# Sample attention rewritten: keys turned by VectorE, block-diagonal queries, 1 MB page gathers, prompt's merge inside the stage

## The reference, cut to what matters

```python
def dilated_window_sample(q, kv_buf, k_new, v_new, window, dilation):
    ...
    sc = jnp.einsum('bqhe,bqjhe->bhqj', q, g[:, :, :, 0]).astype(jnp.float32) * (e ** -0.5)
    p, den, lse = masked_softmax_parts(sc, valid[None, None])
    o = jnp.einsum('bhqj,bqjhe->bqhe', p, g[:, :, :, 1]) / jnp.swapaxes(den, 1, 2)[..., None]

def fox_sample(q, k_new, v_new, logf_new, k_past, v_past, logf_past):
    ...
    s_past = jnp.einsum('bqhe,bkhe->bhqk', q, k_past).astype(jnp.float32) * (e ** -0.5)
    s_past = s_past + cq - jnp.transpose(c_past, (0, 2, 1))[:, :, None, :]
    ...
    pr = jax.nn.softmax(jnp.concatenate([s_past, s_new], axis=-1), axis=-1)

def merge_branches(oa, ob, ga, gb, w_pa, w_pb, w_o):
    ya = oa.reshape(b, s, A_OUT) @ w_pa
    yb = ob.reshape(b, s, B_OUT) @ w_pb
    return (ga * ya + gb * yb) @ w_o
```

## Time and profile before

| | |
|---|---|
| median of 3 runs | 1204.61 us (1200.33 to 1204.88) |
| span of the profiled execution | 1184.3 us; the page has no time of its own beside it |
| median less span | 20.3 us |
| TensorE, VectorE, ScalarE, POOL busy | 1046.9, 333.7, 261.0, 243.6 us |
| `phase_c` | 387.5 to 750 us |
| merge in `phase_d` | 750 to 795 us |

### The profile page before, as it was taken

One profiled execution on the slowest core, in us unless ns is written; L12 is line 12 of the kernel. 1 busy time (PEld: TensorE's weight loads), 2 busy tenths in 40 slices (PEclk: granted clock), 3 DMA queues, 4 the chain that ended last, 5 costly groups with the idle time before them and its releaser, 6 DMA issues. The chain is left out here.

```text
span 1184.3 us, 19295 instructions
## 1 busy us (share of the span) xinstructions
PE 1046.9 (88%) x7440; PEld 641.5 (54%) x7440; DVE 333.7 (28%) x881; ACT 261.0 (22%) x585; POOL 243.6 (21%) x257
## 2 busy tenths in 40 slices
PE   3999999997998699799998999999968998787870
PEld 2444444444565477577776766764545554444430
DVE  3100033226862432122232210232451231000105
ACT  3000000013553132223232221312222111111114
POOL 1000043301200100455403565000013332212110
PEclk9999999999998699899999999999978998889895
DMA  9976666877877889999999986877088999999966
GB/s 330 372 281 251 251 251 251 314 231 248 261 248 248 265 242 292 364 325 353 327 340 342 353 270 205 302 274 310 36 347 290 367 380 384 380 391 380 408 243 239
DMA packets 120726, 353.69 MB, mean 299 GB/s; under 512 B 15578, under 2 KB 59362, under 8 KB 109886
## 3 DMA queue, kind: packets, MB, share of 16 engines
q1 hardware_dynamic: 91166, 289.37, 68.1%
q0 software_dynamic: 16576, 46.42, 11.5%
q10 hardware_dynamic: 12896, 16.69, 4.3%
HBM read 336.38 MB, written 67.55 MB: 341 GB/s over the span
## 5 line engine op out<-in xcount | busy, mean ns | idle before, releaser
L1364 POOL DMA_INDIRECT w_all<-in_cache_b_v,value_rows x128 | 121.1, 946 | 213.7 <-PE bank L1482 128.8
L422 PE MATMUL bank<-w_all,turned 128*128 128x481 f32 (+2 forms) x384 | 119.3, 503 | 1.1 <-DVE turned L640 1.1
L422 PE MATMUL bank<-w_ring,turned 128*128 128x481 f32 (+2 forms) x384 | 118.7, 502 | 0.0
L1391 PE MATMUL bank<-ident,w_all 128*128 128x128 f32 x720 | 100.1, 292 | 19.2 <-DMA w_all<-in_cache_b_k 9.1
L1885 PE MATMUL bank<-w_all,mix_row 128*64 128x256 f32 x736 | 94.6, 415 | 24.8 <-DMA w_all<-in_w_exp 23.7
L1391 PEld LDWEIGHTS bank<-ident,w_all 128*128 128x128 f32 x720 | 85.0, 149 | 33.9 <-DMA w_all<-in_cache_b_k 11.5
L1885 PEld LDWEIGHTS bank<-w_all,mix_row 128*64 128x64 f32 x736 | 62.2, 150 | 63.9 <-issue 44.5
L1629 DVE COPY mods<-bank 128x512 f32<-128x512 f32 x90 | 62.1, 691 | 106.8 <-PE bank L1391 103.0
L422 PEld LDWEIGHTS bank<-w_all,turned 128*128 128x128 f32 (+1 forms) x384 | 56.8, 171 | 61.5 <-issue 58.4
L422 PEld LDWEIGHTS bank<-w_ring,turned 128*128 128x128 f32 (+1 forms) x384 | 57.1, 171 | 60.1 <-issue 56.9
L1566 ACT ACTIVATE mods<-bank 128x512 f32<-128x512 f32 x90 | 53.1, 596 | 100.3 <-PE bank L1391 100.3
(11 more groups left out here) (337 smaller groups left out, 1309.4 us busy)
## 6 DMA issues: line engine op xcount, KB each, us to landing
w_all<-in_w_exp SPq DMA_DIRECT2D x22, 2048.0 KB, 40.4
w_all<-in_cache_b_k SPq DMA_DIRECT2D x128, 256.0 KB
out_a_sample<-in_cache_a SPq DMA_DIRECT2D x8, 4080.0 KB, 20.9
w_all<-in_w_exp SPq DMA_DIRECT2D x25, 1024.0 KB, 38.5
w_all<-in_cache_a SPq DMA_DIRECT2D x96, 256.0 KB, 7.6
mods<-in_w_ada SPq DMA_DIRECT2D x21, 1024.0 KB, 8.1
turned<-in_w_exp SPq DMA_DIRECT2D x5, 2048.0 KB, 42.2
mods<-in_w_exp SPq DMA_DIRECT2D x5, 2048.0 KB
```

What stands on the lines that cost most here:

```text
L422: mm = nc.tensor.matmul(m.banks[i][r:r + ROWS[i], 0:hi - lo], m.hT[:, k, i * P:i * P + ROWS[i]], ring[u][:, CW * k + lo:CW * k + hi], star ...
L1364: pool.indirect_dma_start(out=vr[k % RINGS][2 * j + y], out_offset=None, in_=value_rows, in_offset=bass.IndirectOffsetOnAxis(ap=v_row[:, p ...
L1391: mm = nc.tensor.transpose(T(b)[:, y * P:(y + 1) * P], buf[part][:, c:c + P], m.ident[:, :])
```

## The change

The unit of work becomes a window group or the pages of four sequences (order a, a, b, b). All keys of a unit come first, then all its values: 92 steps, one ring of six places of 1 MB for both. Each page step is one gather by POOL of 128 runs of four rows (8 KB). VectorE turns a granule in blocks of 32x32 and writes it at a step of four floats. Partition 32s + j then holds feature j of sequence s, and the queries stand in a block diagonal (`m.wa`, `m.wb`), so that one product scores four sequences. Gates and the prompt's merge are cut in 88 pieces and spread over steps 3 to 79; tanh takes the sigmoid's place (a factor of two goes into the norm's epsilon); gates stay on chip. w_o and the merge weights for the sample are loaded at the stage's end; `phase_d` begins with w_o of the first tile and merges only the sample's 64 tokens. The last 12 steps use three ring places.

```diff
-KV_RING = 4
+KV_RING = 6
...
+            for u in range(2):
+                for s in range(4):
+                    ins = nc.scalar.activation(m.wa[32 * s:32 * s + 32, u, :, DEC * s:DEC * (s + 1)], own_qa[32 * u:32 * u + 32, :, DEC * s:DEC * (s + 1)],
                                                ACT.Copy, scale=SCALE)
...
+                dve.wait_ge(pool_half, 2 * TILES)
+                dve.wait_ge(dve_half, 2 * TILES)
+                for dst, col, width in ((own_qa, QA, AW), (own_ka, KA, AW), (m.own_b[0:NS, 0], QB, BW)):
+                    nc.vector.transpose(dst, m.qkv[0:NS, last, col:col + width].rearrange("p (f j) -> p f j", j=32)).then_inc(own_t, 1)
...
+            for k in range(1, KV_RING - 1):
+                early_keys(k)
+                piece(BEFORE + 1 + k)
...
-    UNITS = [("a", 0), ("b", 0), ("b", 1), ("a", 1), ("b", 2), ("b", 3)]
+    UNITS = [("a", 0), ("a", 1), ("b", 0), ("b", 1)]
+    COUNT = [7, 7, PAGES, PAGES]
+    STEPS = [(u, part, g) for u in range(len(UNITS)) for part in "kv" for g in range(COUNT[u])]
+    TAIL, TAIL_SLOTS = 12, (4, 5, 0)
+    slot_of = [n % KV_RING if n < N - TAIL else TAIL_SLOTS[(n - N + TAIL) % 3] for n in range(N)]
...
+        parts = [(c, h) for c in (2 * p, 2 * p + 1) for h in range(2)]
+        for c, h in parts:
+            pieces += [("gate", c, h, 0, 0), ("gate", c, h, 0, 4)]
+        pieces.append(("sample", 2 * p, 0, 0, 0))
+        for c, h in parts:
+            pieces += [("gate", c, h, 1, 0), ("gate", c, h, 1, 4), ("out", c, h, 0, 0)]
+        pieces.append(("sample", 2 * p, 0, 1, 0))
+    FIRST, END = 3, 80
...
+        @block.sync
...
+            def gate_weights(p, b):
+                if p:
+                    sp.wait_ge(gate_pe, sums_by(p - 1, b))
...
             sp.dma_start(pt_col[:], I["page_table"].rearrange("a n -> n a")).then_inc(pcol_in, 16)
+            window(KV_RING - 1)
+            gate_weights(0, 0)
             for j in range(4):
                 sp.dma_start(wmask[32 * j:32 * j + 32, :], I["mask_window"]).then_inc(con_in, 16)
             sp.dma_start(consts[:], I["sample_consts"]).then_inc(con_in, 16)
+            gate_weights(0, 1)
+            merge_weights(0)
+            sp.dma_start(page_ids, I["page_table"].rearrange("a n -> (a n)").partition_broadcast(P)).then_inc(pages_in, 16)
...
+                pool.indirect_dma_start(out=m.ring[slot_of[n]], out_offset=None, in_=src,
+                                        in_offset=bass.IndirectOffsetOnAxis(ap=rows, axis=0)).then_inc(arrived(n), 16)
...
+        @block.vector
+            def turn(n):
+                u, _, g = STEPS[n]
+                dve.wait_ge(arrived(n), level[n])
+                if k_num[n] >= 2:
+                    dve.wait_ge(scored, k_num[n] - 1)
+                f = BF if kind(u) == "b" else 8
+                ts = 2 if kind(u) == "a" and g < 6 else 1
+                cols = kt[:, k_num[n] % 2, 0:f * ts * P].rearrange("p (f t i c) -> p t c f i", f=f, t=ts, c=4)
+                rows = m.ring[slot_of[n]][:, 0:f * ts * P].rearrange("p (t c f j) -> p t c f j", t=ts, c=4, f=f)
+                for t in range(ts):
+                    ins = V.transpose(cols[:, t], rows[:, t])
+                ins.then_inc(turned, 1)
...
+                for b, th in enumerate((th_a[i % 4], th_b[i % 2])):
+                    V.scalar_tensor_tensor(th, th, 1.0, BOTH[:, 256 * b:256 * (b + 1)], ALU.add, ALU.mult).then_inc(gated, 1)
+                dve.wait_ge(gated, 2 * i + 2)
+                V.tensor_tensor(mix[c][:, 256 * h:256 * h + 256], th_a[i % 4], th_b[i % 2], ALU.add).then_inc(mixed, 1)
...
+            turn(0)
+            dve.wait_ge(pages_in, 16 * 2)
...
+            dve.wait_ge(con_in, 16 * 5)
+            for t in range(N + 1):
+                for x in piece_at.get(t, []):
+                    if x[0] == "out":
+                        mixing(*x[1:3])
+                if t + 1 < N and STEPS[t + 1][1] == "k":
+                    turn(t + 1)
...
-            for v, (c, half) in enumerate(MERGES):
...
             pe.wait_ge(wo_in, 16 * 3)
             for h in range(2):
-                mix(0, h, KEEP, KD)
+                mix(0, h)
+            pe.wait_ge(wp_in, 32)
+            for c in range(KD):
+                at, cols = c % 4 * 2 * NS, slice(c * P, (c + 1) * P)
+                for k in range(2):
+                    nc.tensor.matmul(m.banks[c // 4][:, at:at + NS], wp[:, k, cols], m.oaS[:, k, :], start=k == 0, stop=k == 1)
```

More of the change, by code:

```diff
@@ L65 @@
 RING = 6
-KV_RING = 4
[L67 to L71, removed]
+KV_RING = 6
+RING_AT = VA + AH * HD
+RING_TILES = (4, 0, 1, 2, 3)
+GRANULE = 2048
+QF, BF = AW // 32, BW // 32
 class Link:
@@ L978, in _ @@
             early(-AHEAD)
-            for c in range(4):
-                mm = nc.tensor.transpose(ADA_BANK[:, c * NS:(c + 1) * NS], m.qkv[0:NS, 4, KB + c * P:KB + (c + 1) * P], m.ident[0:NS, 0:NS])
-            mm.then_inc(own_t, 1)
             for n in range(1 - AHEAD, 0):
@@ new lines, in phase_c, with use @@
+    ends_chunk = lambda u, g: g % 2 == 1 or g + 1 == COUNT[u]
+    uses = []
+    use_at = {}
+    def use(t, when, what, u, x):
+        use_at.setdefault((t, when), []).append(len(uses))
+        uses.append((what, u, x))
+    for t, (u, part, g) in enumerate(STEPS):
+        if part == "k":
+            if g == 1 and u:
+                use(t, "after", "fold", u - 1, 0)
+            continue
+        if kind(u) == "a":
+            if g == 0:
+                use(t, "before", "probs", u, 0)
+                use(t, "before", "probs", u, 1)
+            if g in (1, 3):
+                use(t, "after", "probs", u, g // 2 + 2)
+            if (u, g) == (0, 2):
+                use(t, "after", "totals", u, 0)
+            if g == 4:
+                use(t, "after", "shares", u, 0)
+        else:
+            if g == 0:
+                use(t, "before", "probs", u, 0)
+                use(t, "before", "probs", u, 1)
+            if g % 4 < 2 and g < 12:
+                use(t, "after", "probs", u, 2 * (g // 4 + 1) + g % 4)
+            if g == 10:
+                use(t, "after", "probs", u, 8)
+            if g == 11:
+                use(t, "after", "shares", u, 0)
@@ L1216, in phase_c @@
+    FIRST, END = 3, 80
+    piece_at = {}
+    for n, x in enumerate(pieces):
+        piece_at.setdefault(FIRST + n * (END - FIRST) // len(pieces), []).append(x)
+    step_of = {x: t for t, xs in piece_at.items() for x in xs}
+    items = [x[1:3] for x in pieces if x[0] == "out"]
+    sums = [x for x in pieces if x[0] == "sample" or (x[0] == "gate" and x[4] == 4)]
+    sum_of = {x[0:4]: n for n, x in enumerate(sums)}
+    sums_by = lambda p, b: sum_of[("sample", 2 * p, 0, b)] + 1
     with ExitStack() as ctx:
@@ L1973, in _ @@
             sp.sem_clear(range(ids[0], ids[-1] + 1))
-            for c in range(GB):
-                gates(c)
-            w_o(0, 3)
-            gates(5)
-            w_o(3, 6)
-            gates(6)
-            gates(7)
             for i in range(LAST):
```

1214 lines of the change are left out of this document (604 added, 610 removed).

## The result

The kernel after takes 1228.18 us (median of 4 runs, 1220.67 to 1234.72), the kernel before 1202.47 (4 runs). The ratio is 1.0226, with a 95% interval of 1.0176 to 1.0277. The forecast was 1236, 2.6% slower.

The account below looks back on a forecast made before the run. VectorE's turns were to bound key steps, TensorE value steps; DMA was not the bound. Stage terms summed to 819, 829 with the merge, against 795.2: 34 later, less 2, so 1204.6 + 32 = 1236 us; range 1168 to 1258.

Parts of the forecast that it names:

- Where it is slower: Page key steps of the sample-attention stage: the bound passes to VectorE, 4.6 us a step against TensorE's 3.6.
- The first rival: VectorE turns at one element per cycle whatever the write step, 2.3 us a page step; 43 us less, 1193 us; chance 0.40.
- The price of a turn: VectorE's transpose of a page key step, written at a step of four floats: 3.8 us, priced from copy L1128.
- Start: Stage opening: VectorE waits behind its first turn for page ids SP queues last, TensorE with it, to 411 us.
- the sum: Sample stage added up stretch by stretch, from start 411 us to tail 40 + 5, giving 819 us.
- The tail: Last 12 steps, three ring places: w_o's 4.2 MB beside 9.4 MB of values, 40 us, then 5 us.
- the check of bytes: Sample stage's DMA: some 116 MB at 307 to 384 GB/s, 302 to 378 us in 431, not the bound.
- The 20.3 us of the prediction: Kernel before: median of the runs, 1204.6 us, over the profiled span, 1184.3 us; w_o's shift was added to the median.
- SP's waits for TensorE's pieces: SP's queue of gate and merge weights and window loads: waits name pieces one step back, costed at nothing.
- The dear turn: VectorE's turn as two full passes, 4.5 us a page step; 30 us more, 1266 us; chance 0.08.
- The slow software queue: Tail: one queue with 8 KB rows and three places moves only 307 GB/s, 44 us for 35; 1245 us; chance 0.08.
- The upper-end uncertainty: TensorE's reads at the same step dearer too, for 64 turned probability blocks: 0 to 6 us.

Follow-up runs that it names:

- unit_again: Kernel after, but turned keys written in runs of 32 floats and key order restored in VectorE's bias addition; repeat run, 1197.3 us, ratio 0.9954.
- The ladder: Kernel after plus seven VectorE transposes and copies at different steps, in the hole behind its first turn; 1229.0 us (one run).
- wo_late: Unit-step turns and reordered opening as in start_again, but SP issues w_o at the third-last value step instead of the seventh-last; 1165.2 us, ratio 0.9693.
- start_again: Unit-step turns as in unit_again, plus SP's opening loads reordered and VectorE's waits for ids and constants moved to its first addition; repeat run, 1181.7 us, ratio 0.9823.

## Why the prediction was right, and which of its terms were off

**Where it is slower.** Right. The key steps passed to VectorE at 3.9 us a page turn, and with unit-step writes the kernel is 30 us faster and level with the kernel before. The first rival's condition, turns of 2.3 us, was made by that kernel: it forecast 1193, 12 under the median it started from, and 0.9979 and 0.9954 are 3 and 6 us under. Its 43 us for the turns were too many by 13. That VectorE's saving counts only down to TensorE's own key step was in this sum already; the two steps were closer than priced. From the first to the last page score of a unit (15 steps) it takes 67.1 and 64.7 us in the kernel after, 4.4 a step and not 4.6, and 56.4 and 56.1 in unit_again, 3.75 and not 3.6. So a page step gave 0.65 us instead of 1.0, some 20 of the 32 us.

**The price of a turn.** Right in size (3.8 forecast, 3.90 measured), and less sure in its reason. It was taken from a copy out of PSUM "because the same engine writes there at the same step". The ladder's copy at this step, between places in SBUF, costs 0.97 ns an element and not 1.79. The number was near, but the copy is no proof of a common cause, and that it gave the right price is in part luck; and a step of two floats would have been nearly free.

**Start.** Right: turned keys from 414.8 us (411 forecast), TensorE idle from 390.6 to 418.6 (395 to 411 forecast). The queue of SP made it, and VectorE's waits ahead of its second turn; worth 16 us, since 10 come back as a wait for gate weights.

**Stage by stage.** By the sum, page keys begin at 529, their values at 610, the second page keys at 677, the last values at 758, w_o at 819. Measured: 531, 607, 673, 746 and 818.7. The end fits because terms were off in opposite ways, 13 us too much in the page keys and 12 too little in the last values, and that they cancel is luck:

- The page units' keys took 76 and 73 us with their change to values instead of 81 each. The sum has 76 for 16 steps, though 16 of its own 4.6 are 74. In the second unit VectorE's first turn began at 667.5 us, under the last values, 5.8 ahead of the first score (673.2); the sum has it start with the scores. And its step cost 4.4 us (16 in the 71 us to 738), not 4.6: the mixing passes took 416 ns and not 480.
- The tail was mis-sized. It counted 13.6 MB, w_o and values, and left out the 3.1 MB of merge weights behind w_o in the same queue, although the check of bytes in the same text had them: 8 us at 384 GB/s. Where TensorE waits, its granted clock is 0.5, the 1.2 GHz level, so a value step costs 1.94 us instead of 1.07 and the last fold 7 us. Together the last 12 steps and their end took 58 us (from 761 to 818.7), not 45. What the merge weights cost was tried only together with w_o, in wo_late.

**The number.** 1236 was 8 us above the median of 1228.2: 2 of them because the kernel before took 1202.5 in this result and not 1204.6, 6 because the medians differ by 25.7 and not by 32. The spans of the two profiled executions differ by 34.4, near the 32, but neither is a median execution. The kernel after's took 1220.67, 7.5 below its median. In all later runs of the kernel before, the time stands 1.6 to 1.8 us above the span (1203.4 against 1201.8), so its profiled execution took about 1186, an estimate, some 17 below the median. The 20.3 us of the prediction were thus nearly all the distance of one quick execution from the median. The shift was right for these two executions and 6 us too large for the medians; why the kernel before's execution was so quick stays open.

**TensorE's terms.** The sample's merge took 10.7 us, 10.3 forecast. The 8 records of a half gate sum took 1.92 us (start_again: 407.94 us to the next score at 409.86) where 1.73 was priced. With 64 of them in 77 steps that is 0.16 us a step: a page value step with its piece took 3.48 us (654.93 to 658.41), 3.4 forecast, and TensorE's key step 3.75 where 3.6 was. SP's waits for TensorE's pieces, which the forecast put at nothing, were rightly put there: TensorE waits for no gate weights in the kernel after.

**The other rivals.** The dear turn (4.5 us) is out. The slow software queue gave nearly the right tail: 761 to 818.7 us of the kernel after moved 293 GB/s, under this rival's 307, and took 58 us where it has 54. But its reason is out. From 720 to 730 us of wo_late POOL's queue moved 366 GB/s by itself, with 8 KB rows and three places, and with SP's 7.3 MB out of the way TensorE's waits for those gathers fell from 22.9 to 9.7 us. The upper-end uncertainty, probabilities turned at a step of four on TensorE, was real but small: at the full clock four of these records take 0.75 us where four take 0.66 in the kernel before, so 16 times four cost 1.4 us more.

## What to carry to other kernels

Price an operation by the step at which it writes, and if the order is needed for one consumer only, let the cheapest pass restore it: here an addition that reads PSUM at a step did so for nothing, where the transpose paid 1.6 us each time. List the bytes of a tight stretch by going down the issuing queue, with all that stands behind the named transfer: a prefetch that is issued early takes its bandwidth from the transfers that someone already waits for. And a wait that stands ahead of an engine's urgent work (ids and constants ahead of the second turn) should be moved to the first instruction that needs it, with every other wait beside it.

## What the runs showed of the chip that I had not expected

- VectorE's block transpose slows by its write step, and not in proportion: 1.13 ns an element in runs, 1.22 at two floats, 1.93 at four. A copy in SBUF at four floats takes 0.97 on either side and 0.60 flat. The Trainium skill (Vector Engine (DVE) Microarchitecture Reference, section 3.8) has the transpose array "Pipelined to sustain one element per cycle per lane"; runs of 32 and of 512 floats do share one pace, 1.13 ns, but read as a rule for any write it does not hold here: at four floats the pace is 1.93. How many cycles either is, no run shows.
- TensorE writing its scores in four pieces of 32 columns, 64 floats apart, costs nothing: 273 ns a record of page scores (median) with it and without it.
- With w_o and the values in flight together, 740 to 760 us of start_again ran at 426 and 429 GB/s, above the 384 of the earlier trace rows on which the tail was priced.
